# Unread fp32 products on the TensorE queue of a one-layer hybrid encoder step

## The reference

```python
x = x + 0.5 * (silu(h @ w1_gate) * (h @ w1_up)) @ w1_down      # h = rmsnorm(x) * g_ffn1, D_FF = 2816
h = rmsnorm(x) * g_mix
z = h @ w_in                       # q (8 heads x 64), k, v (2 x 64), mq, mk, mv, mo (4 x 128 each), two gates
q, k = rmsnorm(q) * g_q, rmsnorm(k) * g_k
att = sliding_window_attention(q, k, v, alibi, sinks)           # 64-frame chunks, 192 keys
hl  = rmsnorm(sigmoid(mo) * mlstm(mq, mk, mv, gates)) * g_out   # 4 heads x 128, chunkwise
x = x + concat(att, hl) @ w_out
x = x + 0.5 * (silu(h @ w2_gate) * (h @ w2_up)) @ w2_down      # h = rmsnorm(x) * g_ffn2
y = rmsnorm(x) * g_final                                        # also k, v, C, n, m for the cache
```

## Time and profile before

| | us |
|---|---|
| median of 3 runs | 2359.24 |
| lowest, highest | 2358.8, 2360.32 |
| the profiled execution, its own time | 2356.54 |
| its span in the trace | 2355.0 |
| PE busy | 2171.7 (92%) |
| DVE, ACT, POOL busy | 980.7, 487.5, 163.6 |

### The profile page before, as it was taken

How to read it: one execution, slowest core, us unless ns; L and a number is a source line. 1 busy time by engine, 2 the same in 40 slices (tenths; PEclk the granted TensorE clock), 3 DMA queues, 4 the chain that set the end, 5 groups by cost and what they waited for, 6 DMA issues and landing times.

```text
span 2355.0 us, 31966 instructions
## 1 busy us (share of the span) xinstructions
PE 2171.7 (92%) x12949; PEld 2104.1 (89%) x12949; DVE 980.7 (42%) x1700; ACT 487.5 (21%) x869; POOL 163.6 (7%) x222
## 2 busy tenths in 40 slices
PE   5999999999999987779998479999999999999997
PEld 4999999999999986668887378899999999999997
DVE  3633343433434355644433353363343433343435
ACT  3310111100111023424343242230011110111102
POOL 2100000000000001121121231010000000000000
PEclk8999999999999998889999689999999999999999
DMA  3301111011111010223321451021111101111002
GB/s 112 109 19 36 53 53 53 18 53 36 53 53 43 2 36 24 65 86 91 93 84 40 114 135 37 29 72 46 44 53 53 50 21 36 53 53 53 18 0 85
DMA packets 123221, 127.61 MB, mean 54 GB/s; under 512 B 9944, under 2 KB 110328, under 8 KB 123168
## 3 DMA queue, kind: packets, MB, share of 16 engines
q1 hardware_dynamic: 115472, 107.26, 14.6%
q0 software_dynamic: 7696, 19.63, 2.8%
HBM read 109.27 MB, written 17.54 MB: 54 GB/s over the span
## 4 chain that ended last, share of the span: by engine, by line
PE 52%; issue 35%; DVE 6%; ACT 4%; DMA 1%; POOL 1%; DVEq 0%; SPq 0%; ACTq 0%; POOLq 0%
PE bank L215 15%; PE bank L217 15%; PE bank L216 15%; PE bank L244 2%; ACT SP L844 1%; PE bank L1343 1%; PE bank L1333 1%; PE bank L1352 1%; DMA XIN<-in_x_prompt 1%; DVE SP L1071 1%; DVE YO L1243 1%; ACT L844 0%; DVE RS L250 0%; DVE WGL L310 0%; DVE RSC L1018 0%
## 5 line engine op out<-in xcount | busy, mean ns | idle before, releaser
L215 PE MATMUL bank<-HH,WGH 128*128 128x362 f32 (+1 forms) x2856 | 951.0, 333 | 32.7 <-DVE WGL L310 13.2
L217 PE MATMUL bank<-HH,WGL 128*128 128x362 f32 (+1 forms) x2856 | 942.1, 330 | 0.0
L216 PE MATMUL bank<-HL,WGH 128*128 128x362 f32 (+1 forms) x2856 | 939.3, 329 | 0.0
L215 PEld LDWEIGHTS bank<-HH,WGH 128*128 128x128 f32 x2856 | 542.6, 190 | 44.4 <-issue 37.0
L216 PEld LDWEIGHTS bank<-HL,WGH 128*128 128x128 f32 x2856 | 543.3, 190 | 2.0 <-issue 0.5
L217 PEld LDWEIGHTS bank<-HH,WGL 128*128 128x128 f32 x2856 | 541.8, 190 | 0.0
L357 DVE TENSOR_TENSOR AT<-ST,bank 128x364 f32<-128x364 f32 (+1 forms) x132 | 70.3, 532 | 728.4 <-PE bank L217 728.4
L215 PE MATMUL bank<-AH,WDH 128*128 128x362 f32 (+1 forms) x1056 | 349.1, 331 | 9.9 <-DVE X L369 9.9
L217 PE MATMUL bank<-AH,WDL 128*128 128x362 f32 (+1 forms) x1056 | 347.0, 329 | 0.0
L216 PE MATMUL bank<-AL,WDH 128*128 128x362 f32 (+1 forms) x1056 | 345.6, 327 | 0.0
L369 DVE SCALAR_TENSOR_TENSOR X<-bank,X 128x362 f32<-128x362 f32 (+1 forms) x528 | 276.2, 534 | 155.3 <-PE bank L217 153.0
(11 more groups left out here) (231 smaller groups left out, 1326.4 us busy)
## 6 DMA issues: line engine op xcount, KB each, us to landing
RAWG<-in_w_gate SPq DMA_DIRECT2D x22, 1024.0 KB, 5.3
RAWU<-in_w_up SPq DMA_DIRECT2D x22, 1024.0 KB, 7.8
RAWD<-in_w_down SPq DMA_DIRECT2D x22, 1024.0 KB, 4.8
RAW<-in_w_in SPq DMA_DIRECT2D x22, 512.0 KB, 4.0
ZQ<-zm SPq DMA_DIRECT2D x8, 768.0 KB, 5.1
zm<-ZST POOLq DMA_DIRECT2D x32, 181.0 KB, 2.2
XIN<-in_x_prompt SPq DMA_DIRECT2D x2, 2048.0 KB, 14.1
RAW<-in_w_out SPq DMA_DIRECT2D x8, 512.0 KB, 5.6
```

Of the source, the lines that this page charges most:

```text
L215: nc.tensor.matmul(bank[:, 0:w], w_hi, rhs_hi, start=first, stop=False)
L216: nc.tensor.matmul(bank[:, 0:w], w_hi, rhs_lo, start=False, stop=False)
L217: return nc.tensor.matmul(bank[:, 0:w], w_lo, rhs_hi, start=False, stop=last)
```

## The change

A function `unread` is added. It puts `count` fp32 products of `ONES` (128 x 128) with the first 256 columns of `X` on PE's queue, into the first 256 columns of a bank that holds nothing needed at that time. No semaphore is raised and nothing reads the result. There are five places: 26 products after the norm sums of tile 0 of the first FFN; 8 before the wait for the norm of tile 1 (c = 4) and 8 before that of tile 2 (c = 8) of the mixer; 24 in round c = 19; 10 before the second FFN, behind its wait for the last additions to `X`.

```diff
+        def unread(count, bank):
+
+            for _ in range(count):
+                nc.tensor.matmul(bank[:, 0:256], ONES[:, :], X[:, 0, 0:256], start=True, stop=True)
...
             norm_pe(pe, norm[0], 0, BANK[4])
+            unread(26, BANK[1])
             ffn_pe(pe, ffn[0], norm[0])
...
             for c, (j, n) in enumerate(M1):
                 if c < 12 and c % 4 == 0:
+                    if c:
+                        unread(8, BANK[6])
                     norm_wait(pe, norm[1], n)
                 pe.wait_ge(z.lo, j)
+                if c == 19:
+                    unread(24, BANK[6])
                 if c >= 4:
                     if c - 4 in PLAIN:
                         pe.wait_ge(z.ev, PLAIN.index(c - 4) + 1)
...
             pe.wait_ge(o_add, 3 * OUT_UNITS)
+            unread(10, BANK[5])
             ffn_pe(pe, ffn[1], norm[2])
```

## The result

The changed kernel took 2376.65 us (2374.2 to 2377.75, 4 runs) against 2359.02 us (4 runs) of the kernel before: ratio 1.0078, interval 1.0066 to 1.009, so +17.6 us. It was timed twice more, each time beside its own runs of the kernel before: +15.0 us (1.0069, 1.0056 to 1.0082) and +13.0 us (1.0067, 1.0054 to 1.008), five runs each. The forecast was +14.0. The ratio is not the quotient of the two medians: by the ratios the three differences are +18.4, +16.2 and +15.8 us, and the intervals reach from +12.7 to +21.2.

A forecast was written before the change was run, and what follows sets the result against it. PE's queue, busy 92% of the span, was taken as the bound. Terms -0.8, -0.1, +0.3, +10.3 and +4.3 summed to +14.0 us on 2359.24, giving 2373.2 us, range 2366 to 2380.

The forecast's parts named there:

- Place 4: 24 products in round 19, behind the head sum that waits 12.51 us: none covered, +10.3 us.
- Place 5: 10 products before the second FFN, behind the 0.62 us wait for `X`: nothing won, +4.3 us.
- the small terms: Terms for the blocks before the first FFN chain, chain 4 and chain 8: -0.8, -0.1 and +0.3 us.
- The chain that I followed back from attention to chain 20: Dependencies from the 9.47 us wait ahead of attention back to chain 20 on PE, so the whole 10.3 us counts.
- That rival: Round 19's delay is absorbed in the 12.9 us PE waits ahead of attention: 2362.9 us, chance 0.05.
- the other three: Rivals: clock is all, 2351.6 us (0.02); low clock throughout or double price, 2390.4 (0.04); products dropped, 2359 (0.02).
- the row's price: PE's cost per 256-column product, from the norm sums' records: 0.43 us at full clock, 0.86 at half.
- place 1: 26 products before the first FFN chain, ending 2.1 us ahead of it: between 0 and -1.65 us, middle -0.8.
- places 2 and 3: 8 products each before chains 4 and 8, behind the head sums, partly at low clock: -0.1 and +0.3 us.
- The rule of half the throttled time: Skill's clock penalty, throttled time times one minus granted share: 8.3 us here, without a term for the blocks' own time.
- the 16.6 us: Low-clock time at the first FFN chain and chains 4, 8 and 19: 3.6, 4.5, 4.8 and 3.7 us.

The follow-up runs named there:

- the one execution above: The unedited changed kernel's third timing, 2367.89 us against 2354.91 for the kernel before; its profiled execution took 8.11 us from head sum 3 to the norm sums.
- the last kernel: Kernel before plus blocks in every wait up to the second FFN, chain 0's 4 products moved ahead of the wait for `X`: 2348.99 us against 2359.24, 0.9961.

## Why the prediction was right

**The order of the queue decided it.** The forecast rested on the order of the blocks and the instructions that wait, and this held at all five places. Place 4 was +10.3 and is +10.6 both in the trace and alone in the time; moved ahead of the head sum the same block cost nothing that can be measured. Place 5 was +4.3 and is +4.3 in the trace, +3.7 alone. The sum was near, but in the first set it was 3.6 us off, which is as much as executions of one kernel differ, so the times alone would not bear out the small terms.

**Matmuls go strictly in order** (the Trainium skill, "TensorE: Matmul & The Clock Gate", "What overlaps and what doesn't"): the trace agrees, since the block at place 4 starts at 995.55, behind a head sum that had waited 12.52 us with 24 products ready behind it.

**Nothing took the delay up.** The chain that I followed back from attention to chain 20 holds: the waits of 3.5 and 9.5 us kept their lengths under +10.6 and under +21.1 us. That rival is refuted. So are the other three: the products ran at the row's price (0.43 us at full clock, 48 records in 10.5 us), and they are all there.

**The mis-sized term is place 1.** I took the middle between holding the clock over a gap of some 2 us and losing it; it was lost, and the gain was 0 (0.05 us in the trace) in place of 0.8 us. All five profiles with the block of 26, which leaves 2.0 us of waiting, and the one with 24 products ahead of head sum 17, which leaves 2.07, had a stretch at 0.50 after PE had resumed. With 31 products and no gap the same length was 1.1 us shorter in one profile and 1.6 us shorter in the other three. At places 2 and 3 the low clock fell on the block, as worked out, and the blocks' own time ate the rest; only the one execution above had place 2 at full clock.

**The rule of half the throttled time** (the Trainium skill, "TensorE: Matmul & The Clock Gate", "Terms") would have given -8.3 us. Of it holds what the last kernel shows: with the blocks ahead of the waits, lengths at the places fall by 1.6 (place 1), 2.0 (883.35 to 891.07 is 7.72), 2.5 and 2.3 us, 8.4 in all; this takes in the head sum of chain 17, some 1.2 us at the low clock, which the 16.6 us leave out. As a price of the low clock it agrees with the runs; as a forecast of the change it failed, because it does not ask what the filling costs.

What stays open: whether places 1 to 3 cost 0 or 1 to 2 us, and the 3 us outside the block with 48 products. Short stretches at the low clock come and go from one execution to the next (chain 0 at 4.1 or 5.6 us), which fits the size of both, but I did not show that it is their cause.

## What to carry to other kernels

Filling an engine's idle time with work that nobody reads helps only ahead of the instruction that waits, and costs its full length one instruction later: find the row that carries the idle time, and read in the queue's order on which side of it the filling stands. Fill the wait to within some tenths of a us; a rest of 2 us gave the low clock back. And when some waits are filled and others not, the gain is partly lost behind the others, so fill them all or measure what each brings. A block longer than what is left of the wait is paid like one behind it: count the wait from where the block can start.

## What the runs showed of the hardware

After a gap of 2 us the granted clock went to 0.50 while PE was already at work again: by 47.2 us, 1.0 us after the first FFN chain had started (0.8 to 1.3 us after it in the five profiles with the block of 26), and by 995.7 us, 1.5 us after the head sum. The trace of before has one such fall as well, at 942.3, 0.9 us after a wait of 1.96 us had ended. A gap of 1.85 us ahead of chain 0 went both ways: of the twelve profiles that have it, chain 0 took 4.1 us in three and 5.6 in nine. In the last kernel a gap of 1.35 us (858.03) and those of 0.2 to 0.4 us had no such stretch behind them.
